# Four of 24 conditioning units fetched ahead of the mixer, and gates written as rows through DRAM

## The reference

```python
def first_block(x, ...):                    # block 1, layers l = 0, 1
    proj = x @ w_in[l]                      # 1024 -> 3592 columns
    o_a = gdn_mixer(...)                    # gated delta rule: chunks of 64 tokens, 4 heads
    o_b = moba_mixer(...)                   # causal attention, 8 heads
    x = layer_norm(ALPHA * x + concat(o_a, o_b) @ w_out[l], ...)
    hid = causal_dwconv(x @ w_up[l], ...) + bias
    x = layer_norm(ALPHA * x + (silu(gate) * val) @ w_down[l], ...)

def second_block(x, c, ctx, c_ctx, ada_w, ada_b, ...):
    for i in range(2):
        mod = silu(c) @ ada_w[i] + ada_b[i]         # 1024 -> 6144, for the latent stream
        mod_c = silu(c_ctx) @ ada_w[i] + ada_b[i]   # the same for the context stream
        sh1, sc1, g1, sh2, sc2, g2 = split(mod, 6)  # and sh1c, sc1c, g1c, ... of mod_c
        h = x * (1 + sc1) + sh1
        y = retention_mixer(...) if i == 0 else neighbourhood_mixer(...)
        x = layer_norm(ALPHA * x + g1 * y, ...)     # g1: one gate for each of 1024 channels
        x = layer_norm(ALPHA * x + g2 * sq_relu_mlp(x * (1 + sc2) + sh2, ...), ...)
```

## Time and profile before

| what | us |
|---|---|
| median of 3 runs | 2026.49 (2022.56 to 2031.01) |
| the profiled execution | 2034.51 |
| its span, first to last instruction | 2032.5 |
| PE busy in the span | 1964.4 (97%) |
| DVE busy | 1253.6 (62%) |
| ACT busy | 864.3 (43%) |

### The profile page before, as it was taken

One profiled execution on the slowest core, in us unless ns is written; L12 is line 12 of the kernel. 1 busy time (PEld: TensorE's weight loads), 2 busy tenths in 40 slices (PEclk: granted clock), 3 DMA queues, 4 the chain that ended last, 5 costly groups with the idle time before them and its releaser, 6 DMA issues.

```text
span 2032.5 us, 32449 instructions
## 1 busy us (share of the span) xinstructions
PE 1964.4 (97%) x12659; PEld 1608.8 (79%) x12659; DVE 1253.6 (62%) x2071; ACT 864.3 (43%) x1445; POOL 173.3 (9%) x175
## 2 busy tenths in 40 slices
PE   9998999999889999999999999999999999989997
PEld 8765999787569988777777777888888788667996
DVE  6665787476668865544544478444445833867667
ACT  6442665354436655222322326223222433855442
POOL 2011000001010001000000005000000330313000
PEclk9998999999999999999999999999999999999999
DMA  8598665565977655221222132333323253535652
GB/s 253 165 335 260 178 186 194 157 186 159 358 217 219 188 186 179 78 89 63 83 82 83 63 83 91 96 92 94 102 84 103 83 133 106 82 97 172 201 186 83
DMA packets 327161, 297.25 MB, mean 146 GB/s; under 512 B 35031, under 2 KB 248355, under 8 KB 327057
## 3 DMA queue, kind: packets, MB, share of 16 engines
q1 hardware_dynamic: 322960, 283.22, 46.3%
q0 software_dynamic: 4096, 12.58, 1.8%
HBM read 294.70 MB, written 1.05 MB: 146 GB/s over the span
## 4 chain that ended last, share of the span: by engine, by line
PE 84%; DVE 9%; DMA 2%; ACT 2%; issue 2%; POOL 1%; SPq 0%; DVEq 0%; ACTq 0%; POOLq 0%
PE ps L444 24%; PE ps L446 24%; PE ps L445 24%; PE ps L2089 2%; DMA raw<-in_ada_w 2%; DVE w_lo L426 2%; PE ps L595 1%; DVE npr L2665 1%; PE ps L2534 1%; PE ps L2070 1%; PE ps L1818 1%; ACT w_hi L419 1%; PE ps L489 0%; PE ps L654 0%; DVE small L1867 0%
## 5 line engine op out<-in xcount | busy, mean ns | idle before, releaser
L426 DVE TENSOR_TENSOR w_lo<-raw,w_hi 128x1024 fp32r<-128x1024 f32 x428 | 525.2, 1268 | 335.2 <-ACT w_hi L419 334.9
L419 ACT ACTIVATE w_hi<-raw 128x1024 fp32r<-128x1024 f32 x428 | 428.9, 1052 | 537.5 <-PE ps L444 453.3
L444 PE MATMUL ps<-zt_hi,w_hi 128*128 128x512 f32 (+1 forms) x816 | 274.1, 336 | 6.1 <-DVE zt_lo L1809 2.4
L445 PE MATMUL ps<-zt_lo,w_hi 128*128 128x512 f32 (+1 forms) x816 | 273.1, 335 | 0.0
L446 PE MATMUL ps<-zt_hi,w_lo 128*128 128x512 f32 (+1 forms) x816 | 273.1, 335 | 0.0
L444 PE MATMUL ps<-xt_hi,w_hi 128*128 128x256 f32 x864 | 241.2, 279 | 1.9 <-DVE w_lo L426 1.8
L446 PE MATMUL ps<-xt_hi,w_lo 128*128 128x256 f32 x864 | 240.8, 279 | 0.0
L445 PE MATMUL ps<-xt_lo,w_hi 128*128 128x256 f32 x864 | 240.8, 279 | 0.0
L444 PEld LDWEIGHTS ps<-zt_hi,w_hi 128*128 128x128 f32 x816 | 153.1, 188 | 26.3 <-DVE zt_lo L1809 3.3
L445 PEld LDWEIGHTS ps<-zt_lo,w_hi 128*128 128x128 f32 x816 | 153.4, 188 | 18.2
L446 PEld LDWEIGHTS ps<-zt_hi,w_lo 128*128 128x128 f32 x816 | 153.1, 188 | 18.2
(11 more groups left out here) (388 smaller groups left out, 3311.3 us busy)
## 6 DMA issues: line engine op xcount, KB each, us to landing
raw<-in_mlp_w SPq DMA_DIRECT2D x128, 512.0 KB, 4.5
raw<-in_ada_w SPq DMA_DIRECT2D x96, 512.0 KB, 6.9
raw<-in_w_up SPq DMA_DIRECT2D x88, 512.0 KB, 5.2
raw<-in_w_in SPq DMA_DIRECT2D x56, 512.0 KB, 4.9
raw<-in_ret_w_in SPq DMA_DIRECT2D x48, 512.0 KB, 4.3
raw<-in_w_down SPq DMA_DIRECT2D x44, 512.0 KB, 4.3
raw<-in_nat_w_in SPq DMA_DIRECT2D x24, 512.0 KB, 4.9
raw<-in_w_out SPq DMA_DIRECT2D x16, 512.0 KB, 6.3
```

Source lines behind the costliest of these rows:

```text
L419: nc.scalar.activation(w_hi[:, t, w], raw[:, s, w], ACT.Copy).then_inc(on("w_hi"), act.gives("w_hi"))
L426: nc.vector.tensor_tensor(w_lo[:, t, w], raw[:, s, w], w_hi[:, t, w].bitcast(F32), ALU.subtract).then_inc(on("w_split"), dve.gives("w_split"))
L444: first = nc.tensor.matmul(out_ap, l_hi, r_hi, start=start, stop=False)
L445: nc.tensor.matmul(out_ap, l_hi, r_lo, start=False, stop=False)
```

## The change

Units 0 to 3 of each layer's conditioning no longer pass through `raw`. SP fetches them, after unit 3 of `w_in` and ahead of unit 4, into buffers that the mixer uses later (`v_beta`, `k_bg`, `k_dec`, `kn`, `d_inc`, `d_beta`, `a_mat`, `attn`); in layer 1 it first waits until PE has finished the down projection of layer 0, since those buffers share space with its tensors. PE multiplies them inside the projections, into bank 6, and ACT copies that bank to a buffer of its own, `ada_ahead`. The other 20 units stand in the mixer at a changed `ADA_AT`. `pe_fold` adds the two rows.

The gates are no longer multiplied. Four products (48 columns of `mod` as weights, the identity moving) turn all of `mod`; ACT copies the result once; POOL writes it to a DRAM tensor `gate_rows`; and at four places POOL reads a row of 1024 numbers back into all 128 partitions of `gate_b`.

```diff
@@ sp_layer
             for u in range(6):
+                if u == 4:
+                    if l:
+                        sp.eng.wait_ge(on("y_ps"), sp.takes("y_ps", 8))
+                    for n in range(RAW_SLOTS):
+                        fetch_ada_ahead(sp, l, n)
                 fetch(sp, cols_unit(w_in, 256 * u, 256 * u + P))
...
-            fetch_ada(sp, l, range(ADA_FIRST))
+            fetch_ada(sp, l, range(ADA_AHEAD, ADA_FIRST))
@@ load_ada, fetch_ada_ahead
+            for dst, src in zip(homes, rows_unit(a["ada_w_2"][l], 4 * (n % 2), 512 * (n // 2))):
+                sp.eng.dma_start(dst.rearrange("p (k c) -> p k c", k=2), src).then_inc(on(full), sp.gives(full, 16))
...
+            load_ada(sp, l, n, ada_home[n % RAW_SLOTS])
@@ the table
+        ADA_AHEAD = 4
+        AHEAD_AT = {4: 1, 6: 1, 7: 1, 8: 1}
-                  ("x", 3): 2, ("mb", 1): 1, ("mc", 1): 1, ("x", 5): 1, "u": 1, ("mb", 2): 1, ("mc", 2): 1,
-                  ("ma", 3): 1, ("ws", 1): 1, ("mc", 3): 1, ("ws", 2): 1, ("ov", 2): 1, ("ws", 3): 1}
...
+                  ("x", 3): 1, ("mb", 1): 1, ("mc", 1): 1, ("ma", 2): 1, ("mb", 2): 1, ("mc", 2): 1,
+                  ("ma", 3): 1, ("ws", 1): 1, ("mc", 3): 1, ("ws", 2): 1, ("ws", 3): 1}
@@ pe_fold
-                ins = T.matmul(ps[3][:, 24 * f:24 * f + 24], ada_row[:, hs(f)], cst[:, C_FOLD:C_FOLD + 24],
-                               start=True, stop=True)
+                for row in (ada_ahead, ada_row):
+                    ins = T.matmul(ps[3][:, 24 * f:24 * f + 24], row[:, hs(f)], cst[:, C_FOLD:C_FOLD + 24],
+                                   start=row is ada_ahead, stop=row is ada_row)
@@ pe_mixer
+                pe_ada(pe, AHEAD_AT.get(u, 0))
...
+                    pe_ada(pe, AHEAD_AT.get(6 + 2 * n + j, 0))
@@ act_mixer, in the projections
+                if n == 1:
+                    act.eng.wait_ge(on("ada_used"), ADA_UNITS * l + ADA_AHEAD)
+                    act_copy(ada_ahead[:, :], ps[6][:, :]).then_inc(on("ada_row"), act.gives("ada_row"))
@@ pe_ffn, last layer of block 1
-                        pe_gates(pe, 0, 2, (0, 1))
+                        pe_gate_rows(pe)
@@ the gates
+        def pe_gate_rows(pe):
+            for l in range(DEPTH):
+                for s in range(2):
+                    ins = T.matmul(ps[4][0:48, hs(2 * l + s)], mod[:, l, :, s], ident, start=True, stop=True)
...
+        def pool_gate_rows(pool):
+            pool.eng.wait_ge(on("gate_t"), pool.takes("gate_t"))
+            pool.eng.dma_start(gate_rows.rearrange("n c p -> c n p"),
+                               gate_t[0:48, :].rearrange("c (n p) -> c n p", n=4)).then_inc(
+                                   on("gate_row"), pool.gives("gate_row", 16))
+            pool.eng.wait_ge(on("gate_row"), pool.given("gate_row"))
...
+        def pool_gates(pool, n):
+            l, chunk, streams = GATES[n]
             for s in streams:
+                row = gate_rows[2 * l + s, 8 * chunk:8 * chunk + KT, :]
+                pool.eng.dma_start(gate_b[:, s, :], row.rearrange("k p -> (k p)").partition_broadcast(P)).then_inc(
+                    on("gate_b"), pool.gives("gate_b", 16))
@@ gpsimd, end of block 1 and block 2
                 if l + 1 == DEPTH:
+                    pool_gate_rows(pool)
                     pool.eng.wait_ge(on("y_ps"), pool.takes("y_ps", 8 * DEPTH - 2))
                     eng.dma_start(xc[:, :, :], ...)
+                    pool_gates(pool, 0)
                 pool_norm(pool)
...
                 pool_stream(pool, ALL)
+                pool_gates(pool, 1 + m)
             pool_nat(pool)
...
             pool_stream(pool, LAT)
+            pool_gates(pool, 3)
```

More of the change, by code:

```diff
@@ L389, in fetch_ada @@
                     sp.eng.wait_ge(on("ada_used"), ADA_UNITS * l + held + 1)
-                for half, src in enumerate(rows_unit(a["ada_w_2"][l], 4 * (n % 2), 512 * (n // 2))):
-                    dst = raw[:, s, half * 1024:(half + 1) * 1024].rearrange("p (k c) -> p k c", k=2)
-                    sp.eng.dma_start(dst, src).then_inc(on(f"ada_full{u % RAW_SLOTS}"), 16)
+                load_ada(sp, l, n, [raw[:, s, half * 1024:(half + 1) * 1024] for half in range(2)])
         def after_ada(sp, l, n):
@@ L580, in build @@
         ADA_FIRST = 16
         def ada_slot(u):
-            n = u % ADA_UNITS
-            return (14 + u // ADA_UNITS * (18 + FT + FT // 2) + u + (2 if n >= ADA_FIRST else 0)) % RAW_SLOTS
+            l, n = u // ADA_UNITS, u % ADA_UNITS
+            m = n - ADA_AHEAD
+            return (14 + l * (18 + FT + FT // 2 + ADA_UNITS - ADA_AHEAD) + m + (2 if n >= ADA_FIRST else 0)) % RAW_SLOTS
         def pe_ada(pe, n):
             for _ in range(n):
-                u, j = pe.atom, pe.atom % 2
-                g, s = pe.atom % ADA_UNITS // 2, ada_slot(pe.atom)
+                n, j = pe.atom % ADA_UNITS, pe.atom % 2
+                g, ahead = n // 2, n < ADA_AHEAD
+                bank = ps[6] if ahead else ps[5]
+                if ahead:
+                    halves = ada_home[n % RAW_SLOTS]
+                else:
+                    s = ada_slot(pe.atom)
+                    halves = [raw[:, s, half * 1024:(half + 1) * 1024] for half in range(2)]
+                full = f"ada_full{n % RAW_SLOTS}"
@@ L592, in pe_ada @@
                 pe.atom += 1
-                pe.eng.wait_ge(on(f"ada_full{u % RAW_SLOTS}"), 32 * (u // RAW_SLOTS + 1))
+                pe.eng.wait_ge(on(full), pe.takes(full, 32))
                 for k in range(4):
-                    ins = T.matmul(ps[5][32 * k:32 * k + 32, :], cs[:, 4 * j + k, 22 - 2 * g:54 - 2 * g],
-                                   raw[:, s, 512 * k:512 * k + 512], start=g == j == 0,
-                                   stop=g == ADA_UNITS // 2 - 1 and j == 1)
+                    ins = T.matmul(bank[32 * k:32 * k + 32, :], cs[:, 4 * j + k, 22 - 2 * g:54 - 2 * g],
+                                   halves[k // 2][:, 512 * (k % 2):512 * (k % 2) + 512], start=n in (0, ADA_AHEAD),
+                                   stop=n in (ADA_AHEAD - 1, ADA_UNITS - 1))
@@ L653, in pe_warm @@
             for _ in range(n):
-                T.matmul(ps[6][:, :], a_mat[:, 0, 0:P], a_mat[:, 0, :], start=True, stop=True)
+                T.matmul(ps[6][:, :], x_inv[:, 0, 0:P], x_inv[:, 0, :], start=True, stop=True)
         def pe_params(pe):
@@ L707, in pe_mixer @@
             release(pe)
-            assert sum(ADA_AT.get(step, 0) for step in ["begin", "u", *mixer_steps()]) == ADA_UNITS
+            assert sum(ADA_AT.get(step, 0) for step in ["begin", *mixer_steps()]) == ADA_UNITS - ADA_AHEAD
             pe_ada(pe, ADA_AT["begin"])
@@ L2227, in dve_head @@
                 dve.eng.wait_ge(on("xc_in"), dve.takes("xc_in", 16))
-                dve.eng.wait_ge(on("gate_b"), dve.takes("gate_b", 4))
+                dve.eng.wait_ge(on("gate_b"), dve.takes("gate_b", 32))
                 for c in range(2):
@@ L2348, in step @@
                                 up(j)
-                            pe_gates(pe, l, 5, streams)
                         else:
@@ L2705, in dve_nat @@
                 split_lo(dve)
-            dve.eng.wait_ge(on("gate_b"), dve.takes("gate_b", 2))
+            dve.eng.wait_ge(on("gate_b"), dve.takes("gate_b", 16))
             open_hh(dve)
```

59 lines of the change are left out of this document (26 added, 33 removed).

## The result

| | us |
|---|---|
| changed kernel, median of 4 runs | 2040.33 (2039.14 to 2043.74) |
| kernel before, median of 4 runs | 2024.53 (2020.37 to 2031.01) |
| ratio | 1.0066, 95% interval 1.004 to 1.0093 |
| profiled execution of the changed kernel | 2039.14, span 2037.4 |

The forecast was 2015, range 2004 to 2024. The change made the kernel slower: by 13.4 us by the ratio, by 15.8 by these two medians, and by 11.1 against the 29 later runs of the kernel before that the experiments use (2029.26). The time is outside the range.

The account below looks back on a forecast made before the run. PE, busy nearly all the span, was taken as the bound, with DMA waits in block 1's mixers. Gates -9.5, norm +0.4, mixers -8.2, clock counted back +2.5, start +3.5 sum to -11.3: from 2026.5 to 2015, range 2004 to 2024.

Parts of the forecast that it names:

- The gates, -9.5: All four gate places: 96 product records removed, 10.4 us, less 0.9 for turning `mod`; gain bounds 6 and 10.4.
- The start, +3.5: Layer 0's projections: eight DMAs ahead of unit 4 of `w_in` delay it to 40.9; PE wants it at 37.4.
- the rival with 0.22: Rival: the clock falls at the start behind PE's wait, costing 5.1 us, total 2020; chance 0.22.
- The "Slower" rival: Start: SP issues the eight DMAs 4.91 us each, PE stands 32 us, total 2049; decides from about 3.4 a DMA; chance 0.06.
- the price of 7 us: Start: PE's wait for unit 4 if the eight DMAs move at 294 GB/s, the rate there now, instead of 389.
- The mixers, -8.2: Block 1's two mixers: four units fewer shrink PE's DMA waits; layer 0 -5.6, layer 1 -2.6; bounds -16 and 0.
- unit 16, +1.1 in each layer: Mixers: unit 16's fetch, behind both halves of `w_out`, lands at 138.2 when PE is there at 137.1.
- The clock of layer 0's mixer, -5.1 and half counted back: Layer 0's mixer: its clock loss of 5.1 goes; +2.5 counted back since the typical run may lack the fall.
- The base: Profiled execution 2034.51 against median 2026.49, 8.0 less; the clock's fall, perhaps missing from typical runs, would be most of that.
- the norm at the end of block 1: End of block 1: two gate loads issued by POOL delay the first power for the last norm, +0.4, between 0 and 1.4.
- layer 1's start: Layer 1's projections: the same eight DMAs end by 414, PE wants unit 4 at 431; cost 0.
- the gates' path through DRAM: Write, wait and six 512 KB loads on POOL: gates lie ready long before use, so it costs nothing by itself.

Follow-up runs that it names:

- experiment 1: The kernel before with only the gates' part of the change (rows through DRAM, no gate products): 2026.62 us, ratio 0.9987.
- experiment 3: The changed kernel, with layer 0's four units fetched behind w_in's units 7 to 9, not ahead of unit 4, and multiplied later in both layers: 2031.66 us, ratio 1.0016.
- Experiment 5: The changed kernel with the late fetch in layer 0, plus w_out's two units fetched behind conditioning unit 17 instead of 15: 2028.87 us, ratio 0.999.
- experiment 2: The kernel before with only the four conditioning units' part of the change, gates multiplied as before: 2040.03 us, ratio 1.0057.
- experiment 4: The changed kernel with the gates' products put back in the first units of the two MLPs, results unused: 2037.13 us, ratio 1.0036.
- experiment 6: The changed kernel with late fetch and later w_out, plus the gates' products put back in both MLPs' first units, results unused: 2025.38 us, ratio 0.9982.
- Experiment 7: The changed kernel with POOL's pass over the stream at the start of both MLPs cut to 1 column of 1024: 2029.0 us.
- experiment 8: The changed kernel with late fetch and later w_out, plus POOL's stream pass in the first MLP started later: 2021.2 us, ratio 0.9965.

## Why the prediction was wrong

**The gates, -9.5: half right in mechanism, wrong in size.** The step that failed is "All stand between weight products on a full PE, so I count them whole". Block 1's 32 records did (-2.6, as worked out), and so did the 16 of the neighbourhood mixer (-1.8). The 48 of the MLPs did not. In the first MLP they stood ahead of PE's wait for `hh_lo`, 1.0 us in the trace of before, and DVE behind that wait was the slower engine: from 1240.53 to 1263.15 it was busy for 19.6 of 22.6 us, with one idle stretch of 2.98. A wait that ends on DVE right behind the products meant that they were cover: PE's wait grew by 3.5, to 4.5 us, for 3.5 us of products removed. I had priced this as a lower bound ("3.5 us of it as lost at worst") and taken the other end. The row that tells why stood in the trace of before too: DVE's splits of 6.7 us under POOL's pass, which I had taken for a share to be lost instead of the bound itself:

```profile
1240.53 6.71 DVE L426 TENSOR_TENSOR w_lo<-raw,w_hi 128x1024 fp32r<-128x1024 f32 x2 [0.26 <-ACT w_hi L419]
```

The bound held for the products but left out what came on top, the clock: it fell at that wait in the profiles of the changed kernel and of experiments 1, 3 and 5, all with a wait of 3.0 us or more, and not in those of before, 2, 4, 6 and 7, with 1.2 at most, nor at the 1.6 us of experiment 8. A short wait is no guarantee: in experiments 1 and 8 the clock fell once more at the MLP's start, behind idle stretches of 0.74 and 1.22 us; before has 0.84 and 1.22 us there and no fall. Experiments 1, 4, 6 and 7 show it from three sides: gates alone -2.6 instead of -9.1, products back -3.2 and -3.5, pass away -11.3.

**The start, +3.5: right place, right transfer, two sizes off.** Landing times came out to the tenth (38.7, 40.6). The step that failed is "ACT and DVE need 1.0 and 1.2 us for a half: 40.9", counted from the first half, as if ACT could begin with it. ACT waits for both, so PE starts 2.2 us later, and the stop is 5.5. The other is the clock: the rival with 0.22 was what happened, at about half its price of 5.1 (6.9 us at the lower level, 5.1 of them with PE at work, 2.6 lost). The two make 8.1 of the 8.5 us in the trace, and experiment 3 gives 8.7. The forecast's 3.5 with the rival's 5.1 would have been 8.6: near by luck, since one is too small and the other too large. The "Slower" rival had the right side and the right place, but the wrong pace: SP issued the eight at 1.2 us apart, not 4.91. Its limit of 3.4 us a DMA was wrong too. By its own terms the stop is eight times the pace less 7.2 us, and with 5.1 of slow clock it eats the other 14.8 us of gain from a pace of 2.1. And the 294 GB/s of the price of 7 us is 301 in rows 10.

**The mixers, -8.2: the mechanism failed.** The step is "Units 17 to 23 now find the queue drained, since each fetch starts one to two steps earlier". From unit 18 on the fetches do not follow the uses. Unit 18's slot holds a unit of `w_out`, and that is split where ACT's and DVE's lists have it, at `x` 5 and behind `mb` 2. In the changed kernel unit 18 was issued at 159.2, in the one before at 147.8, with the mixer itself 12.6 us later: not one or two steps earlier but at the same step, within 1.2 us. Four units less ahead of that gate only made the DMA engines idle in front of it (0.47), and in layer 0 three DMA waits took the place of two. I had read the landings of the queue and not who opens it. Experiment 5 moves the gate by two units, and the waits are gone.
What I charged for unit 16, +1.1 in each layer, came as 0.6 and 0.5. The clock of layer 0's mixer, -5.1 and half counted back, was worth about 3.4 us there, as an estimate: it was low for 10.2 us in before's profile and for 3.4 in that of the changed kernel, and half of the difference is 3.4. That is more than the -1.6 of the whole row, and in layer 1 two falls came on top. So of the -8.2 no gain in the waits is left that the runs can show: in layer 1, where the DMA waits fell by 1.4 us, the mixer without a fall of the clock is shorter by its four units and no more, so other idle time took their place.

**The base.** The profiled execution of before was 8 us over its median, and I laid that to its clock. In that same execution the products of layer 0 from 235 us on also stood wider apart, which makes 5.6 us against the changed kernel. Either could be the 8 us, and no run tells which, so the half that I counted back for the clock had no ground.

**Right:** the norm at the end of block 1 (+0.4; +0.5 measured), layer 1's start (no wait at its unit 4), the gates' path through DRAM (no wait of DVE on it).

## What to carry to other kernels

A product is worth its time only where the next wait behind it is not on another engine; look one wait further than the removed instruction, and if it ends on an engine that is the slower one there, the product is cover and its removal buys idle PE, and may cost clock. In a queue through shared slots, ask of each fetch which event opens it and where that event stands in its engine's list; work taken out ahead of a fixed gate does not move what is behind the gate. Bytes put in front of a transfer that is needed soon delay it by their whole transfer time where the DMA engines are full already (4.2 MB, 10.8 us here), and a unit is ready for an engine that waits for all of it only with its last half. A stretch with a fall of the clock in one profile and not in the other tells little of the change; look for profiles without one.

## What was not expected of the hardware

**Two spacings of the same products at the same granted clock.** From 240 to 320 us the rows of the kernel before, the changed kernel and experiment 1 are

```profile
240.00:320.00 80.00, 80.00 (x682) 80.00 (x681) 66.41 (x114) 51.67 (x86) 0.00 (x0) 1.00 0.68 190
```

```profile
240.00:320.00 80.00, 80.00 (x708) 80.00 (x707) 68.87 (x117) 53.05 (x90) 0.00 (x0) 1.00 0.70 192
```

```profile
240.00:320.00 80.00, 80.00 (x708) 80.00 (x708) 68.65 (x119) 53.69 (x88) 0.00 (x0) 1.00 0.68 191
```

682 against 708 records in 80 us of full PE with a granted clock of 1.00, by the same code: 4.5 ns more from one product to the next, 0.118 against 0.113 us. Within one execution it changes between stretches (products of 512 columns: 0.233 and 0.229). Experiment 5's profiled execution had the slow one in this stretch and was 5 us longer for it. What sets it is open; it was not tried. Experiment 7's had it too. It may be part of why runs of one kernel lie 14 to 21 us apart.
